# Half of the value rows of a gathered expert layer summed on TensorE instead of VectorE, with PSUM stages cut from eight banks to six

## The reference

```python
eidx = (e1 * PEER_NKEYS + e2).reshape(T, PEER_HEADS * PEER_TOPK)     # 128 expert numbers per token
gates = jax.nn.softmax(sc, axis=-1).reshape(T, PEER_HEADS * PEER_TOPK)
...
act = jax.nn.gelu(jnp.einsum('td,tkd->tk', xt, peer_u[it]), approximate=False)
return jnp.einsum('tk,tkd->td', gt * act, peer_v[it])
```

## Time and profile before

| | |
|---|---|
| median of 3 runs | 3450.09 us (3436.97 to 3450.14) |
| the profiled execution, its own time | 3448.32 us |
| its span, first to last instruction | 3447.0 us |
| TensorE busy (matmul) | 70% |
| VectorE busy | 55% |
| GpSimd busy | 38% |
| ScalarE busy | 13% |
| mean granted TensorE clock | 0.724 of full speed |
| DMA | 761.89 MB, mean 221 GB/s |
| gathers | 1024 issues from GpSimd, 539.79 MB |

### The profile page before, as it was taken

One profiled execution on the slowest core, in us unless ns is written; L12 is line 12 of the kernel. 1 busy time (PEld: TensorE's weight loads), 2 busy tenths in 40 slices (PEclk: granted clock), 3 DMA queues, 4 the chain that ended last, 5 costly groups with the idle time before them and its releaser, 6 DMA issues. The chain is left out here.

```text
span 3447.0 us, 25459 instructions
## 1 busy us (share of the span) xinstructions
PE 2413.4 (70%) x8594; PEld 1672.6 (49%) x8594; DVE 1903.6 (55%) x3694; ACT 431.7 (13%) x1194; POOL 1311.0 (38%) x1041
## 2 busy tenths in 40 slices
PE   6998940356857633002739999499518999999998
PEld 3736730224525513001437668285215766678763
DVE  1412159878676678998779866766672222211100
ACT  1201000002101000000003220021000222220100
POOL 0000004677465877337678657654640000000000
PEclk9797975675667866555855559799859555569999
DMA  4221416798687999668899879999963100004342
GB/s 156 72 85 49 159 39 195 260 378 308 219 346 275 402 351 355 201 214 327 326 400 335 275 226 350 386 383 401 402 241 118 44 1 0 1 27 157 130 156 93
DMA packets 259169, 761.89 MB, mean 221 GB/s; under 512 B 22000, under 2 KB 28576, under 8 KB 258528
## 3 DMA queue, kind: packets, MB, share of 16 engines
q0 software_dynamic: 148416, 539.79, 42.9%
q1 hardware_dynamic: 107328, 215.88, 17.3%
q10 hardware_dynamic: 3296, 4.60, 0.4%
HBM read 758.10 MB, written 2.10 MB: 221 GB/s over the span
## 5 line engine op out<-in xcount | busy, mean ns | idle before, releaser
L304 POOL DMA_INDIRECT picks_rows<-peer_u_dram,expert x512 | 686.2, 1340 | 828.0 <-DVE expert L1439 522.6
L304 POOL DMA_INDIRECT picks_rows<-peer_v_dram,expert x512 | 617.3, 1206 | 413.6 <-DVE h L367 300.9
L367 DVE SCALAR_TENSOR_TENSOR h<-picks_rows,picks_weight,h 128x1024 f32<-128x1024 f32 x512 | 654.9, 1279 | 101.0 <-DMA picks_rows<-peer_v_dram,expert 80.9
L361 DVE CUSTOM_DVE_ANT_0 picks_rows<-picks_rows,xn 128x1024 f32<-128x1024 f32 x512 | 615.0, 1224 | 165.8 <-DMA picks_rows<-peer_u_dram,expert 161.9
L635 PE MATMUL psum<-identity_sb,n_scaled 128*128 128x128 f32 (+1 forms) x104 | 23.6, 411 | 399.8 <-DVE n_scaled L620 399.8
L445 PE MATMUL psum<-weight_ring,hnT 128*128 128x512 f32 (+4 forms) x576 | 236.3, 572 | 23.4 <-DMA weight_ring<-w_in_dram 11.9
L445 PE MATMUL psum<-xn,weight_ring 128*128 128x256 f32 x1024 | 222.9, 381 | 8.9 <-DVE xn L601 8.9
L1725 PE MATMUL psum<-weight_ring,aT 128*128 128x512 f32 x512 | 220.8, 593 | 3.2 <-DMA weight_ring<-w_ff_dram 1.3
L635 PEld LDWEIGHTS psum<-identity_sb,n_scaled 128*128 128x128 f32 (+1 forms) x104 | 20.2, 224 | 403.8 <-issue 362.8
L445 PEld LDWEIGHTS psum<-xn,weight_ring 128*128 128x128 f32 x1024 | 195.4, 191 | 36.3 <-issue 9.6
L929 DVE TENSOR_REDUCE na_negmax<-psum 128x1 f32<-128x15 f32 (+5 forms) x192 | 73.8, 384 | 239.4 <-PE psum L834 239.3
(11 more groups left out here) (332 smaller groups left out, 3260.8 us busy)
## 6 DMA issues: line engine op xcount, KB each, us to landing
weight_ring<-w_in_dram SPq DMA_DIRECT2D x36, 2048.0 KB, 17.7
weight_ring<-w_ff_dram SPq DMA_DIRECT2D x32, 2048.0 KB, 14.1
weight_ring<-w_ret_out_dram SPq DMA_DIRECT2D x4, 2048.0 KB, 7.9
weight_ring<-w_mix_out_dram SPq DMA_DIRECT2D x4, 2048.0 KB, 17.3
weight_ring<-w_peer_q_dram SPq DMA_DIRECT2D x4, 2048.0 KB, 13.2
picks_rows<-peer_u_dram,expert POOLq DMA_INDIRECT x512, 8.5
picks_rows<-peer_v_dram,expert POOLq DMA_INDIRECT x512, 6.2
weight_ring<-w_proj_nsa_dram SPq DMA_DIRECT2D x4, 2048.0 KB, 7.9
```

The source lines that it names most:

```text
L304: pool.indirect_dma_start(out=self.rows[:, n % GATHERS, :], out_offset=None, in_=table, in_offset=bass.IndirectOffsetOnAxis(ap=self.expert ...
L361: ins = nc.vector.tensor_tensor_reduce(out=row, in0=row, in1=self.x[t], scale=1.0, scalar=0.0, op0=ALU.mult, op1=ALU.add, accum_out=self.d ...
L367: ins = nc.vector.scalar_tensor_tensor(out=h, in0=row, scalar=self.weight[:, t % 2, k:k + 1], in1=h, op0=ALU.mult, op1=ALU.add)
```

## The change

`on_pe(k)` returns True for odd k, so 64 of the 128 v steps of each tile go to TensorE by way of the diagonal matrix that GpSimd builds. `BANKS` goes from 8 to 6, so that banks 6 and 7 belong to the accumulation; the attention stage thereby has one bank for values. Adding the two banks into `h` becomes `fold`, two `tensor_tensor` of 128x512 per tile on VectorE, which runs before the next tile's `make_weights` or in `finish`. The places where TensorE does its picks (`picks.add`) are moved or made more: before the waits of a norm or gate stage, after each source of a transpose stage, behind the scores of an attention item and not at its end, inside the compress stage, and after each tile's product in the lower MLP stage. The number of turns of the compress and lower MLP stages grows; the steps per stage stay as they were.

```diff
-BANKS = 8
+BANKS = 6
 V_BANKS = (6, 7)
...
 def on_pe(k):
 
-    return False
+    return k % 2 == 1
...
             if table is not self.peer_u and self.weights == t:
+                if t:
+                    self.fold(dve, t - 1)
                 self.make_weights(dve, t)
...
         self.add_to(pe, end)
+        self.fold(dve, t)
+        self.finished += 1
+
+    def fold(self, dve, t):
+
+        end = 2 * PICKS * (t + 1)
+        pe_picks = self.owner[:end].count("pe")
+        if self.folded > t or not pe_picks:
+            return
+        self.folded = t + 1
         dve.wait_ge(self.taken["dve"], self.dve_done_by(end))
-        pe_picks = self.owner[:end].count("pe")
-        if pe_picks:
-            dve.wait_ge(self.taken["pe"], pe_picks)
-            for c, bank in enumerate(V_BANKS):
-                h = self.g.h[:, t, 512 * c:512 * c + 512]
-                self.g.nc.vector.tensor_tensor(h, h, self.g.psum[:, bank, :], ALU.add).then_inc(self.sum_added, 1)
-        self.finished += 1
+        dve.wait_ge(self.taken["pe"], pe_picks)
+        for c, bank in enumerate(V_BANKS):
+            h = self.g.h[:, t, 512 * c:512 * c + 512]
+            self.g.nc.vector.tensor_tensor(h, h, self.g.psum[:, bank, :], ALU.add).then_inc(self.sum_added, 1)
...
@@ norm_stage, tensor
             for t, (_, rows, _) in enumerate(sources):
+                g.picks.add(pe, t)
                 pe.wait_ge(*s_scaled.after(t + 1))
...
@@ turn_stage, tensor
             mm.then_inc(s_turned.sem, 1)
+            g.picks.add(pe, n + 1)
...
@@ attention_stage, tensor
                         mm.then_inc(s_scores.sem, 1)
+                g.picks.add(pe, min(i, n_items))
                 if i >= late:
...
-                g.picks.add(pe, min(i, n_items))
             g.picks.add(pe)
...
@@ mlp_down_stage, tensor
                     mm.then_inc(g.w.products_done, 1)
-                g.picks.add(pe, groups * b + k)
+                    g.picks.add(pe, n_tiles * (groups * b + k) + t + 1)
```

More of the change, by code:

```diff
@@ L280, in __init__ @@
         self.first = self.last = self.turn = self.turns = 0
-        self.activated = self.weights = self.finished = 0
+        self.activated = self.weights = self.finished = self.folded = 0
     def share(self, tag, turns):
@@ L1519, in compress_stage @@
     names = [("ck1", "second", run), ("cv1", "second", run)]
-    g.open(tag, 3)
+    g.open(tag, 6)
     with ExitStack() as ctx:
@@ L1540, in tensor @@
                     mm.then_inc(g.w.products_done, 1)
+                    g.picks.add(pe, 2 * x + j + 1)
             for x in range(2):
@@ L1548, in tensor @@
                 mm.then_inc(s_out.sem, 1)
-            g.picks.add(pe, 2)
+            g.picks.add(pe, 5)
             pe.wait_ge(*s_roped.after(1))
@@ L1563, in scalar @@
                                          ACT.Gelu_apprx_tanh).then_inc(s_hidden.sem, 1)
-                g.picks.activate(act, x + 1)
+                g.picks.activate(act, 2 * x + 2)
             g.picks.activate(act)
@@ L1569, in vector @@
             link = linker(dve, s_link)
-            g.picks.use(dve)
+            for _ in range(4):
+                g.picks.use(dve)
             dve.wait_ge(*s_out.after(1))
@@ L1633, in tensor @@
             g.begin(pe)
+            g.picks.add(pe, n)
             pe.wait_ge(*s_diff.after(1))
@@ L1711, in mlp_down_stage @@
     name = lambda b, k: (("ff2", b, k), "second", run)
-    g.open(tag, 2 * groups)
+    g.open(tag, 2 * groups * n_tiles)
     def sync(sp):
@@ L1736, in vector @@
         for b in range(2):
-            for k in range(groups):
+            for _ in range(groups * n_tiles):
                 g.picks.use(dve)
```

## The result

The changed kernel takes 3555.99 us (median of 4 runs, 3549.58 to 3587.83) against 3447.24 for the kernel before (4 runs, 3436.97 to 3450.14). The ratio is 1.0345, 95% interval [1.0312, 1.0378]: slower by 3.4% (the two medians alone give 1.032). The forecast was 3429 us; the time lies inside its range, on the side of rivals (a) and (b). The profiled execution took 3549.58 us, its span is 3548.3 us and its mean granted clock 0.824 of full speed (0.724 before).

What follows compares the result with a forecast made beforehand. It took the flow of 1024 steps as the bound, with VectorE limiting only the selection stages; -50 + 5 - 6 + 4 + 12 + 5 + 6 + 5 = -19 us gave 3429 us, range 3362 to 3594.

Steps and rivals of the forecast that it cites:

- (a): Rival, chance 0.22: TensorE stays at the low clock in the attention stages, which become the bound; 3708 us, or 3569.
- (b): Rival, chance 0.13: diagonals wait out VectorE steps and GpSimd becomes the bound; 165 us more, 3594.
- 2 drain: Drain, 1552 to 1595: 28 steps, 14 moved; GpSimd's 48 us exceeds the present 43, so +5 us.
- 7 to 9 together: Fold +6 us, GpSimd held at changes from u to v +5, last stretch without picks 0.
- Step 6: MLP, 2238 to 2550: DMA share 1.02, upper half's 18 moved steps fit; +5 us behind the last weights only.
- Step 4: Retention, 928 to 1075: 38 moved steps fill TensorE's 147 us exactly; +4 us taken, between -15 and +33.
- Step 3: First block's attention, 797 to 928: 26 moved steps, clock may rise; -6 us taken, between -26 and +54.
- Step 5: Second block's attention, 1821 to 2055: 59 moved steps, full clock taken, 246 us, +12; +202 at half clock.
- (c): Rival, chance 0.17: clock rises through all attention and retention and the pauses shrink; 67 us less, 3362.
- Step 1: Selection, 1342 to 1552: 43 moved steps take 54 us off VectorE, leaving 151; -50 us taken.
- Step 7: Fold: eight adds of 0.684 us and, where `finish` waits for TensorE, its last step; +6 us.
- Step 9: Last 883 us without picks: one value bank costs 0; without cover some 0.3 us for each of 96 items.

Runs made afterwards that it cites:

- e8_onevalue: Kernel before, eight banks and coarser turns kept, with only the attention's second value bank taken away: 3495.64 us, ratio 1.016.
- e1_rest: Changed kernel with no step given to TensorE, no diagonals and no fold; six banks, one value bank and finer turns stay: 3483.74 us, ratio 1.014.
- e2_half: Changed kernel with only one of the two TensorE products of each moved step: 3515.89 us, ratio 1.0231.
- e3_nodiag: Changed kernel without diagonals: TensorE multiplies moved rows by the plain identity and waits for the gather alone: 3481.88 us, ratio 1.0132.
- e4_lag1: Changed kernel with each diagonal built one gather after its step's own, not five: 3518.2 us, ratio 1.0209.
- e10_lag1_half: Changed kernel with diagonals one step behind the gather and only one of two products per moved step: 3472.16 us, ratio 1.0099.
- e5_selection: Changed kernel with only the 43 odd steps of the selection stages on TensorE, six banks and one value bank kept: 3467.41 us, ratio 1.0087.
- e9_actdiag: Changed kernel with only the 43 selection-stage steps on TensorE, eight banks, and diagonals built by ScalarE instead of GpSimd: 3395.89 us, ratio 0.9867.

## Why the prediction was wrong, point by point

| step | forecast us | measured us |
|---|---|---|
| 1 selection | -50 | -30 |
| 2 drain | +5 | +7 |
| 3 first block's attention | -6 | +29 |
| 4 retention | +4 | +34 |
| 5 second block's attention | +12 | +4 |
| 6 MLP | +5 | +68 |
| 7 to 9 together | +11 | +7 |
| sum | -19 | +119 |

The measured column is the length of the stages after less that before. For 7 to 9 it is what is left of the 119. Its largest piece is a stretch of u steps between the drain and the second attention, which took 225 us before and 238 after. It took 238 in e8_onevalue too, which changes nothing there, so this piece is not shown to be the change's.

**Step 6 failed most.** It had TensorE's load wrong, and with it what bounds the MLP. It set the 18 moved steps of the upper half against TensorE's own work and found room, and that half indeed went from 163 to 161 us. For the lower half it charged only "behind the last weights" and never made the sum for its 41 steps. It read the upper half's 160 us as "in truth 110.75 of work". But the earlier trace rows have 625 records there, and that work has 512; the rest are the lower half's products, done ahead of time. Their own rows, before and then after:

```profile
L1725 PE MATMUL psum<-weight_ring,aT x256: 592/592/697, 2351.6 to 2463.0; 128*128 128x512 f32 x128
```

```profile
L1740 PE MATMUL psum<-weight_ring,aT x256: 592/592/1061, 2438.2 to 2633.8; 128*128 128x512 f32 x128
```

VectorE's first step of the lower half is at 2401 us before and at 2433 after. So TensorE was 49 us ahead of it, with 115 of the 256 records done, and is not ahead at all once it has steps of its own among its products, each of which waits for a gather and a diagonal. It is the moved steps that do this: e1_rest, with all else changed, still has 105 records done ahead, and e2_half, e3_nodiag and e4_lag1 have one or none (e10_lag1_half 19). Over the whole MLP TensorE's busy time before (160.5 + 62.3 = 223 us) and 59 x 1.72 = 101 us make 324 in a time of 312, so +12 even without a gap, where the prediction had +5. In the lower half alone, with nothing done ahead, 16 turns of 16 records are 110 us by the dense stream of the earlier trace rows and 41 x 1.72 is another 70, together 180 us in a stage of 149. The DMA share of 1.02 had kept me from making TensorE's sum in a stage that the DMA bounds. The runs put the stage at 193 with the queue order mended (e4_lag1) and at 220 with it as written.

**Step 4 failed on the way between the queues.** It made the sum (65 on top of 82 us "fills the 147 us exactly") and then took +4, as if a full TensorE could be fed without gaps; it was busy for 149 of 181 us. The +33 at its upper end was the right size, though for another reason: the clock was at 0.91 to 0.95, and most of the time went into the link between queues (e4_lag1 takes 21 us off, e3_nodiag 26). Half of the added products gone took off 4 us (e2_half, 176.9), but the clock fell to 0.79 with them, so this does not tell what TensorE's own time costs there. The 13 us that stay in e4_lag1 are open.

**What both lack** is that the moved steps put one more reader into GpSimd's ring of rows. Before, VectorE alone released slots, and VectorE was never away for long. The prediction asked what some of the engines' sums would be and how dear a diagonal is, not who releases the slot that the next gather waits for.

**Step 3** has two errors. Of +29 us, 15.5 are there with no step moved (e1_rest): the value bank. The prediction had the mechanism but looked at it in the last stretch alone, where nothing else stands in VectorE's queue and the cost is indeed nothing. Its words "were the cover gone, some 0.3 us for each of 96 items" (29 us) name the right place with the wrong price: what an item waits for is not the output's 0.28 us but up to two steps ahead of it. The attention with picks was the row to look at, and the price is 45 to 49 us over both blocks (e8_onevalue, e5_selection). The other 14 us go with the moved steps: with one product of two (e2_half) 10 of them are gone; their cause was not taken further apart.

**Step 5 was right, mechanism and size**: 246 us forecast, 237.5 measured, clock 0.99. TensorE's own part is 234.8 - 59 x 1.72 = 133 us instead of 231.5, a factor of 0.58 where 0.62 was assumed. That the clock would rise was a choice between two levels that no row before could settle. The value bank does not show here: TensorE waits for VectorE's outputs for 0.9 us in all, where it was 26 in e1_rest, and VectorE has half of its steps less, which is the likely reason. Rival (a) did not happen in any attention stage (the clock in the first block's went from 0.50 and 0.55 to 0.77 and 0.82). Rival (c) had the clock right, but in the first block the rise was eaten up by the moved steps.

**Step 1 was too large by 20 us, 11 to 15 of them from the diagonal.** The assumed 0.35 us is 0.63 when nothing is in the way, and 0.84 on average:

```profile
L322 POOL TENSOR_SCALAR picks_diag<-identity_sb,picks_weight x256: 592/626/2736, 787.3 to 2659.0; 128x128 f32<-128x128 f32 x128
```

The pause behind it is 0.17 us, less than assumed. The rest of the price is rival (b)'s mechanism, at a quarter of its size. The timeline after shows a diagonal that starts just after a VectorE step, and one that starts alone:

```profile
966.51 1.28 DVE L369 SCALAR_TENSOR_TENSOR h<-picks_rows,picks_weight,h 128x1024 f32<-128x1024 f32 x1 [2.85 <-DMA picks_rows<-peer_v_dram,expert]
966.58 1.69 POOL L322 TENSOR_SCALAR picks_diag<-identity_sb,picks_weight 128x128 f32<-128x128 f32 x1
...
973.42 0.62 POOL L322 TENSOR_SCALAR picks_diag<-identity_sb,picks_weight 128x128 f32<-128x128 f32 x1
```

66 of the 256 diagonals began while one of VectorE's v steps (L369, two operands in SBUF) was running; they took 1.32 us on average, which is the 0.85 us that was left of that step and 0.47 us, while the other 190 took 0.67. The rule of the Trainium skill (SBUF — State Buffer, two separate sides), by which such a pair excludes each other, agrees with these rows. The estimate of 0.2 us and a dispatch for a diagonal, scaled down from the 769 ns for 512 elements of the Trainium skill (GPSIMD Engine Reference, Performance versus the Vector engine), is a third of the price without the dispatch: 0.59 us is the shortest. Without any diagonal selection took 168.6 us (e3_nodiag), and with ScalarE's, 0.40 us each and outside GpSimd's queue, 165 (e9_actdiag): price and place of the build held 11 to 15 of the 20 us. VectorE's floor of 151 in the prediction shows as 154 busy in e9; the rest is its idle time.

**Step 7** came out as said: eight adds of 0.683 us, 5.1 us, and a wait of 3.4 us for TensorE's last product before the final pair (7.0 us in two such waits in all). **Step 9**: from VectorE's last step to the end it was 887.7 us after, of which 4.7 are that wait and the final pair, 883.4 before, and 881 to 888 over the experiments, with one value bank or two.

## What to carry to other kernels

Before work moves to an engine that is "idle on average", sum that engine's own work and the moved work in each stage, also in stages that something else bounds today, and count in what it now does ahead of time in an earlier stage: with work that waits among its own it may lose that lead. Ask also which slots it must now release and for whom. Move only where the engine that gives is the bound and the one that takes is idle (here 43 of 256 steps: 0.8 to 1.3% faster, where all of them made it 3.4% slower). A second buffer is worth what can stand ahead of the instruction that frees it in an in-order queue, not what that instruction takes.

## What was not expected of the hardware

- Less work took longer: with one product of two (e2_half) the second attention took 251.7 us at a granted clock of 0.74; with both products it took 237.5 at 0.99, and with none of them, at 0.50, 266.8 with one value bank (e1_rest) and 234.0 with two. TensorE was 90 to 99% busy in all of them.
- The stretch from 120 to 172 us, ahead of every gather, ran at 0.93 to 0.97 in the profiled executions of after and six of the experiments and at 0.51 in those of e2_half, e3_nodiag and e4_lag1, though after and e4_lag1 differ in nothing ahead of the first diagonal. It is worth about 18 us, half as much as the times of the kernel before spread in one group of runs (3426.71 to 3461.86). What decides it was not tried.
- Building a diagonal is cheaper on ScalarE (0.40 us) than on GpSimd (0.63 alone, 0.84 on average over the changed kernel).

Some things stay open. Whether all 256 moved steps with two value banks would cost less was not tried, since two banks of PSUM are taken by the sums. Lag 1 in the kernel with the 43 steps, which would tell the diagonal's price from its place there, was not tried either. And 13 us of the lower half of the MLP (e10_lag1_half), 13 of retention (e4_lag1) and some 14 of the first block's attention remain without a shown cause.
